# Moving the activation tiles of a three-pass matmul kernel to other SBUF addresses modulo 256

## The reference

```python
def swiglu(h, w_gate, w_up, w_down):
    return (jax.nn.silu(h @ w_gate) * (h @ w_up)) @ w_down
...
    for layer in range(DEPTH):
        x = x + 0.5 * swiglu(rmsnorm(x, norm_gain[layer, 0]), ...)
        h = rmsnorm(x, norm_gain[layer, 1])
        if layer % 2 == 0:
            x = x + conv_sparse_attn_mixer(h, cos, sin, ev_w_in[i], ...)
        else:
            x = x + gated_deltanet_mixer(h, od_w_in[i], ...)
        x = x + 0.5 * swiglu(rmsnorm(x, norm_gain[layer, 2]), ...)
    return rmsnorm(x, final_gain)
```

## Time and profile before

| | |
|---|---|
| time, median of 2 runs | 2126.68 us (2125.46 to 2127.89) |
| the profiled execution | 2128.9 us, span 2127.1 us |
| mean granted clock of TensorE | 0.994 |
| instructions | 25713, of them 9598 matmuls |

### The profile page before, as it was taken

How to read it: one execution, slowest core, us unless ns; L and a number is a source line. 1 busy time by engine, 2 the same in 40 slices (tenths; PEclk the granted TensorE clock), 3 DMA queues, 4 the chain that set the end, 5 groups by cost and what they waited for, 6 DMA issues and landing times.

```text
span 2127.1 us, 25713 instructions
## 1 busy us (share of the span) xinstructions
PE 2074.7 (98%) x9598; PEld 1713.7 (81%) x9598; DVE 1036.8 (49%) x1542; ACT 775.4 (36%) x1087; POOL 311.1 (15%) x392
## 2 busy tenths in 40 slices
PE   8999999999999999999999999989999999999998
PEld 6888888777777888888788888868788887888887
DVE  4444444489744444433344443266666654444423
ACT  4333322333644323322332322255554543233222
POOL 2000000343221000000000000046565210000001
PEclk9999999999999999999999999999999999999999
DMA  4333322463122333322233232122232222322321
GB/s 171 96 99 99 112 96 81 116 162 89 60 70 89 99 97 92 116 96 86 88 99 98 91 121 98 67 87 81 56 91 56 70 94 94 99 93 94 119 96 54
DMA packets 61884, 200.39 MB, mean 94 GB/s; under 512 B 12496, under 2 KB 14576, under 8 KB 61808
## 3 DMA queue, kind: packets, MB, share of 16 engines
q1 hardware_dynamic: 59168, 198.72, 29.5%
q10 hardware_dynamic: 2640, 0.65, 0.1%
HBM read 188.58 MB, written 2.38 MB: 90 GB/s over the span
## 4 chain that ended last, share of the span: by engine, by line
PE 80%; DVE 7%; POOL 4%; ACT 3%; DMA 3%; issue 2%; SPq 1%; DVEq 0%; ACTq 0%; POOLq 0%
PE prod L496 25%; PE prod L498 25%; PE prod L497 25%; DMA blk<-blocks 2%; POOL rows_tmp L1697 2%; POOL rows L1700 2%; PE misc L740 1%; DVE top L1332 1%; ACT w_hi L905 1%; DVE raw L1333 1%; PE misc L687 1%; DVE w_lo L1206 1%; SPq L460 0%; DMA blocks<-a_mat 0%; PE prod L563 0%
## 5 line engine op out<-in xcount | busy, mean ns | idle before, releaser
L1206 DVE TENSOR_TENSOR w_lo<-raw,w_hi 128x1024 fp32r<-128x1024 f32 (+1 forms) x290 | 381.6, 1316 | 768.6 <-ACT w_hi L905 768.1
L496 PE MATMUL prod<-h_hi,w_hi 128*128 128x512 f32 x1848 | 739.8, 400 | 3.6 <-DVE w_lo L1206 3.2
L498 PE MATMUL prod<-h_hi,w_lo 128*128 128x512 f32 x1848 | 722.9, 391 | 0.0
L497 PE MATMUL prod<-h_lo,w_hi 128*128 128x512 f32 x1848 | 721.9, 391 | 0.0
L905 ACT ACTIVATE w_hi<-raw 128x1024 fp32r<-128x1024 f32 (+1 forms) x316 | 354.9, 1123 | 572.3 <-PE prod L498 558.5
L496 PEld LDWEIGHTS prod<-h_hi,w_hi 128*128 128x128 f32 x1848 | 348.5, 189 | 76.2 <-issue 5.1
L498 PEld LDWEIGHTS prod<-h_hi,w_lo 128*128 128x128 f32 x1848 | 348.2, 188 | 74.2
L497 PEld LDWEIGHTS prod<-h_lo,w_hi 128*128 128x128 f32 x1848 | 348.6, 189 | 70.5 <-issue 2.9
L496 PE MATMUL prod<-a_hi,w_hi 128*128 128x512 f32 x682 | 265.3, 389 | 0.0
L497 PE MATMUL prod<-a_lo,w_hi 128*128 128x512 f32 x682 | 265.3, 389 | 0.0
L498 PE MATMUL prod<-a_hi,w_lo 128*128 128x512 f32 x682 | 265.3, 389 | 0.0
(11 more groups left out here) (284 smaller groups left out, 1888.8 us busy)
## 6 DMA issues: line engine op xcount, KB each, us to landing
raw<-in_w SPq DMA_DIRECT2D x252, 512.0 KB, 3.5
raw<-in_wd SPq DMA_DIRECT2D x64, 704.0 KB, 4.0
blk<-blocks SPq DMA_DIRECT2D x8, 512.0 KB
x<-in_x SPq DMA_DIRECT2D x8, 256.0 KB, 5.3
k_dup<-act_f SPq DMA_DIRECT2D x8, 256.0 KB, 4.1
k_dup<-silu_g SPq DMA_DIRECT2D x8, 256.0 KB, 4.1
silu_g<-g_rows SPq DMA_DIRECT2D x7, 256.0 KB, 4.7
out<-y_out SPq DMA_DIRECT2D x12, 128.0 KB, 1.8
```

The source lines that it names most:

```text
L496: pe.matmul(bank, wh, hi, start=first and k == 0, stop=False)
L497: pe.matmul(bank, wh, lo, start=False, stop=False)
L498: ins = pe.matmul(bank, wl, hi, start=False, stop=last and k == tiles_n - 1)
L1206: dve.tensor_tensor(w_lo[:, n % 2, 0:w], raw[:, n % 4, 0:w], w_hi[:, n % 2, 0:w].bitcast(F32), ALU.subtract).then_inc(lo_ready, 1)
```

## The change

It moves tiles and nothing else. A gap of 192 bytes ahead of `h_hi` and one of 64 behind `h_lo` put the normed tiles 192 bytes on and leave `raw`, `w_hi` and all that follow at the same residue (all 256 bytes further). The `ffn` plan begins 96 bytes into the region, the `ev` plan 160 bytes. Every engine has the same instructions in the same order.

```diff
 ALIGN = 256
+H_OFF, A_OFF, MIX_OFF = 192, 96, 160
...
         x = sb("x", [KT, T])
+        sb("gap0", [H_OFF // 4])
         h_at = (nc.sbuf_base + 31) // 32 * 32
         h_hi, h_lo = sb("h_hi", [KT, T], F32R), sb("h_lo", [KT, T], F32R)
...
+        sb("gap1", [(ALIGN - H_OFF) // 4])
         raw = sb("raw", [4, HALF * P])
...
-        assert region0 % ALIGN == w_at % ALIGN == h_at % ALIGN
+        assert region0 % ALIGN == w_at % ALIGN == (h_at - H_OFF) % ALIGN
...
         ffn = Plan()
+        ffn.at += A_OFF
         a_hi, a_lo = ffn("a_hi", [FT, T], F32R), ffn("a_lo", [FT, T], F32R)

         ev = Plan()
+        ev.at += MIX_OFF
         emix_hi, emix_lo = ev("emix_hi", [KT, T], F32R), ev("emix_lo", [KT, T], F32R)
```

## The result

The changed kernel takes **2174.17 us** (two runs, 2173.38 and 2174.96) against 2126.68: the ratio is 1.0217, with a 95% interval of 1.0200 to 1.0234. It is slower by 47.5 us. The forecast of 2127 was wrong. Whether the loss is over 2% is not decided, since the interval begins there.

A forecast was written before the change was run, and what follows sets the result against it. PE's float32r matmul stream was taken to bound the kernel; span 2127.1 + 0 us, 1.8 around it and 2.2 off for the median gave 2127 us, with a range of 2055 to 2180.

The forecast's parts named there:

- What bounds the kernel: PE's stream of float32r matmuls sets the end, at 0.2267 us each; no other engine presses.
- part 1: Relative address of moving and stationary operand, 7950 matmuls of 512 columns: zero taken, between -91 and +35 us.
- three reasons: Why unequal residues were priced at zero: same excess at both widths, other engines' accesses cost nothing, families alike at different addresses.
- The first: Each matmul takes 13.3 ns beyond its columns, at 512 and 256 alike; an address collision would be unlikely to match.
- The second: In the gate and up window, other engines' SBUF accesses don't disturb the pace by a nanosecond, so places seem irrelevant.
- The third: `emix`, `a`, `h` and `omix`, at base addresses up to 100 KB apart, all take 389 or 400 ns a matmul.
- rival "faster": The 13.3 ns are a collision of two operand reads that distance avoids: in full 2036 us; chance 0.34, 0.22 beyond 2%.
- rival "slower": Gate, up and down units: unequal residues have no resting point or a worse one; 35 us, 2162; chance 0.26.
- bound from above: All 7950 matmuls at the slowest spacing seen behind a norm, 0.24 us: +106 us.
- The three families differ: The offsets act differently: `h` gaining 5 ns and `a` losing 5 ns would give 2109 us; no chance of its own.
- Parts 2 and 3: ACT and DVE writing tiles at other residues: zero. Transfers of `y_out` and stacked keys: zero, bound of one us.

The follow-up runs named there:

- e2_a_and_mix: Against the kernel before, only the tiles of the down projection (96 bytes) and of the attention layer (160) were moved: 2141.85 us, ratio 1.0066.
- e5_swapped: Against the kernel before, `h` moved by 96 bytes, `a` by 192, attention's mixed tiles by 32, DeltaNet's by 160: 2169.96 us in a single run.

## Why the prediction went as it did

*What bounds the kernel* was right: PE's float32r stream sets the end, and nothing else moved when it slowed down. By the prediction's 7.95 us for each ns of pace, 46.1 us are 5.8 ns; the settled pace rose by 6.67, and the matmuls at disturbances by less.

*The value taken for part 1 is the step that failed.* It put the price of unequal residues at zero, with a chance of 0.40 on no effect or one under 6 us. At the distances of `h` and `a` it is 6.67 ns a matmul of 512 columns in the settled stretches. None of the three reasons could carry that. The first said that a meeting of two streams would not cost the same 13.3 ns at 256 columns. But at 192 bytes the 256 columns took 113.4 ns and the 512 columns 233.3, that is 6.7 and 20 ns over their columns: both extras depend on the residue, and that they agree at zero says nothing. The second, that DVE's, ACT's and the transfers' accesses disturb nothing, is true in the changed kernel as well, but says nothing of TensorE's own two reads. The third was no evidence at all, since the four families at their base addresses were all at the same residue. The row that did speak was the one quoted against it: in the earlier trace rows the extra varies with history while the instruction doesn't, so it can't be a constant of the instruction.

Two readings of rows were off, without touching the sum. The LDWEIGHTS that starts 0.01 us behind a matmul in the earlier trace rows isn't its own: behind L497 at 641.85 stands the load of L498, the next matmul. And a plain float32 product shows as two matmuls (L862 x2 in the earlier trace rows, for one line of the program), so that the whole of it takes 0.43 us, four cycles a column; the 215 ns are those of one of the two. In the rival "faster", 3 ns would give 2103, not 2105.

From the lines of 16 bytes and the second read port that the Trainium skill gives (page "SBUF — State Buffer", section "SBUF: two separate sides", and its specifications) the prediction concluded that the offsets change nothing, which agreed with that zero. The measurement disagrees with the conclusion: 192, 96 and 160 bytes are multiples of 16 and cost 6.7 to 7.6 ns, and even 16 bytes cost 5.

*The rival "slower"*, which had a chance of 0.26, is what happened, in mechanism more than in size. It named the place (every gate, up and down unit) and the mechanism (the equal residues let the stream settle at 226.7, others have a worse resting point or none), and priced it by the disturbed stretch at 231.1: 35 us, 2162 with some 3 less. The stream does settle, at 233.33. The bound from above, 0.24, was not reached. That the time lies in the range is partly luck: its end of 2180 stood for 6.7 ns on all 7950 matmuls, which is what the settled ones lost, and only those at disturbances, which lost less, kept the kernel 6 us below it. The mechanism was put in the words "may be no such resting point, or a worse one"; the runs say the second. What went unforeseen is that a disturbed stretch, which passes through all kinds of timings, is faster than the settled cycle of an unequal residue.

*The rival "faster"* has no support at 512 columns: of the nine distances tried, and of twelve mixed placements, none brought a family below 226.67. The 87 us less that the prediction estimated for a stream at 215.7 ns has none either. At 256 columns it did happen, by 6.6 ns at 192 bytes, which is 0.9 us for the 132 of them.

*"The three families differ"* was dismissed rightly for 192 and 96 (both 233.33); 160 costs 0.9 ns more than they do, in all three kernels that had it (the changed one, `e2_a_and_mix` and `e5_swapped`).

*Parts 2 and 3* were right: DVE 1226 against 1237 ns, ACT 1060 against 1070, and the 1.8 us around the span are unchanged.

*What it leaves open.* The relation of moving operand and weights modulo 256 is shown as the cause. Why a family settles at just these values isn't. The settled sums of three matmuls lie mostly on a grid: 680.0 ns with equal residues, 686.7 (3 x 228.9) at 64 and in four mixed placements, 693.3 (3 x 231.1) in four others, 700.0 at most distances, which are steps of 6.67 ns or 16 cycles; but paces of 231.66, 231.9, 232.6 and 234.2 are off it. That suggests meetings of the two reads that cost 6.67 ns each, some number of them in three matmuls. No run measured such a meeting by itself, and neither simple pairing of a load with a matmul survived, so this remains an argument. Why the 256 columns go the other way is open too.

## What to carry to other kernels

In a stream of float32r matmuls of 512 columns whose weights are loaded for each of them, put the moving operand and the weights at the same address modulo 256, all halves of a split alike. Here that is worth 2.2% of the whole kernel and 2.9% of the pace, and it costs a few bytes of padding. At 256 columns the equal residues were not the best, and no run moves the operands of another data type. To see it in a profile, count matmuls in a window without waits, or take the differences of their starts; no wait, no idle time and no other engine shows it. When a trace holds only one case of something (here: equal residues everywhere), that other instances agree is no evidence that it doesn't matter.

## What the runs showed of the hardware

- The settled spacing of 128x512 float32r matmuls with a 128x128 load each was 226.67 ns with equal residues, 228.9 at 64 bytes, 231.7 at 16, 233.3 at 32, 96, 128, 192 and 224, and 234.2 at 160, with the clock at its top level; it repeated after 256 bytes, and moving both operands by 96 bytes didn't change it.
- Matmuls of 128x256 behaved in another way: 120.0 ns at 0, 120.0 at 96, 113.4 at 192, and 113.3 or 117.8 at 64.
- Behind a disturbance the stream ran through spacings of mostly 224 to 236 ns before it settled; with equal residues at one constant spacing, else in a cycle such as 231 and 236.
- Reads and writes of VectorE, ScalarE and the transfers didn't move the settled spacing by a nanosecond in the kernel before (226 and 227 ns throughout from 700 to 900 us), and the cycle of 231 and 236 went on unchanged beside them in the changed one.
